# A fourth bank for the weight stream before the first attention, and modulation pieces moved between engines

## The reference, cut to what matters

```python
def first_block(...):                    # x: (1, 256, 1024) float32
    cond = jax.nn.silu(c)
    for l in range(DEPTH):               # DEPTH = 2
        mod = cond @ w_ada[l] + b_ada[l] # (1, 6 * 1024)
        sh1, sc1, g1, sh2, sc2, g2 = [m[:, None, :] for m in jnp.split(mod, 6, axis=-1)]
        h = _layer_norm(x) * (1.0 + sc1) + sh1
        mix = _mixer(h, w_in[l], ...)
        x = _layer_norm(DN_ALPHA * x + g1 * mix, ln1_g[l], ln1_b[l])
        h = _layer_norm(x) * (1.0 + sc2) + sh2
        ffn = _moe(h, w_router, router_bias, w_exp_gate[l], w_exp_up[l], w_exp_down[l])
        x = _layer_norm(DN_ALPHA * x + g2 * ffn, ln2_g[l], ln2_b[l])
    return x

def _mixer(h, w_in, qn_g, kn_g, w_pa, w_pb, w_o, cos, sin, slopes):
    proj = h @ w_in                      # 1024 -> 5120
    qa, ka, va, qd, kd, vd, gates = jnp.split(proj, IN_SPLITS, axis=-1)
    qa = _apply_rope(_rms_norm(qa, qn_g), cos, sin)
    ka = _apply_rope(_rms_norm(ka, kn_g), cos, sin)
    out_a = _global_gqa(qa, ka, va)
    ...                                  # out_b: three dilated groups, merged by their log-sums
    g_a, g_b = jnp.split(jax.nn.sigmoid(gates), 2, axis=-1)
    merged = g_a * (out_a @ w_pa) + g_b * (out_b @ w_pb)
    return merged @ w_o
```

## Time and profile before

| | us |
|---|---|
| median of 3 runs | 1646.46 |
| lowest, highest | 1646.29, 1647.08 |
| the profiled execution | 1647.17 |
| its span in the trace | 1645.4 |

### The profile page before, as it was taken

How to read it: one execution, slowest core, us unless ns; L and a number is a source line. 1 busy time by engine, 2 the same in 40 slices (tenths; PEclk the granted TensorE clock), 3 DMA queues, 4 the chain that set the end, 5 groups by cost and what they waited for, 6 DMA issues and landing times.

```text
span 1645.4 us, 16703 instructions
## 1 busy us (share of the span) xinstructions
PE 1516.3 (92%) x7088; PEld 856.8 (52%) x7088; DVE 532.2 (32%) x995; ACT 339.9 (21%) x735; POOL 178.4 (11%) x88
## 2 busy tenths in 40 slices
PE   5999889999789999989989998999988998999985
PEld 2777766444358777545436444434325764443322
DVE  2452235521366143551242034121104354221113
ACT  3113230312121223031123123111102243111101
POOL 0009970000000640000000000000002000000000
PEclk8999999799889999989989998999999999999998
DMA  9766453789646642379955524999998433899994
GB/s 387 291 268 243 158 220 139 295 349 418 288 155 262 236 190 103 135 299 375 416 232 204 180 103 160 424 425 427 428 427 352 154 112 149 338 427 428 427 428 197
DMA packets 34569, 462.71 MB, mean 281 GB/s; under 512 B 4432, under 2 KB 4560, under 8 KB 6160
## 3 DMA queue, kind: packets, MB, share of 16 engines
q1 hardware_dynamic: 31376, 447.34, 66.8%
q0 software_dynamic: 3104, 14.12, 2.7%
HBM read 458.29 MB, written 3.15 MB: 280 GB/s over the span
## 4 chain that ended last, share of the span: by engine, by line
PE 77%; DMA 15%; DVE 4%; ACT 1%; issue 1%; SPq 0%; DVEq 0%; ACTq 0%
PE work L739 15%; PE work L557 12%; DMA ring<-in_stream 9%; PE work L540 7%; PE work L792 7%; PE acc L557 7%; DMA area<-in_stream 6%; PE acc L540 5%; PE work L696 4%; PE acc L774 3%; PE work L549 3%; PE work L1218 2%; PE acc L1363 2%; PE work L1021 1%; PE work L757 1%
## 5 line engine op out<-in xcount | busy, mean ns | idle before, releaser
L739 PE MATMUL work<-ring,area 128*64 128x512 f32 x832 | 186.2, 594 | 10.7 <-DMA ring<-in_stream 10.6
L557 PE MATMUL work<-ht_sb,ring 128*128 128x256 f32 x640 | 145.0, 387 | 1.3 <-DMA ring<-in_stream 1.3
L557 PEld LDWEIGHTS work<-ht_sb,ring 128*128 128x128 f32 x640 | 122.9, 194 | 23.4 <-issue 4.4
L739 PEld LDWEIGHTS work<-ring,area 128*64 128x64 f32 x832 | 58.4, 137 | 129.7 <-issue 108.6
L557 PE MATMUL acc<-ht_sb,ring 128*128 128x256 f32 x512 | 115.7, 385 | 4.4 <-DMA ring<-in_stream 4.4
L2343 DVE SCALAR_TENSOR_TENSOR area<-area,comb_slot,work 128x256 f32<-128x256 f32 (+1 forms) x32 | 19.6, 614 | 299.1 <-ACT area L1586 299.1
L557 PEld LDWEIGHTS acc<-ht_sb,ring 128*128 128x128 f32 x512 | 97.3, 192 | 20.9 <-DMA ring<-in_stream 4.8
L739 PE MATMUL work<-area 128*64 128x512 f32 x448 | 100.9, 594 | 7.2 <-DMA area<-in_stream 7.1
L2355 DVE TENSOR_TENSOR area_r<-work,area_r 128x512 fp32r<-128x512 f32 x64 | 44.3, 692 | 173.2 <-ACT area_r L1594 140.7
L475 POOL TENSOR_TENSOR ring<-ring,silu_c 128x4096 f32<-128x4096 f32 x10 | 70.2, 7016 | 180.6 <-DMA ring<-in_stream 180.6
L792 PE MATMUL work<-area 128*64 128x512 f32 x384 | 89.2, 607 | 0.0
(11 more groups left out here) (318 smaller groups left out, 1930.3 us busy)
## 6 DMA issues: line engine op xcount, KB each, us to landing
ring<-in_stream SPq DMA_DIRECT2D x138, 2048.0 KB, 11.7
area<-in_stream SPq DMA_DIRECT2D x55, 2048.0 KB, 12.4
cst<-in_stream SPq DMA_DIRECT2D x19, 2048.0 KB, 16.8
ln_sb<-in_ln_vecs POOLq DMA_DIRECT2D x8, 1024.0 KB, 11.3
rel_rows<-mt_sb POOLq DMA_DIRECT2D x1, 2048.0 KB, 50.8
cst<-in_consts POOLq DMA_DIRECT2D x1, 1465.5 KB, 8.7
x_sb<-in_x SPq DMA_DIRECT2D x1, 1024.0 KB, 16.0
area<-rel_rows POOLq DMA_DIRECT2D x8, 128.0 KB, 2.9
```

What stands on the lines that cost most here:

```text
L557: ins = pe.matmul(dst, w[:, k, c0:c0 + n], src[:, k0 + k, :], start=k == 0, stop=k == ks - 1)
L739: ins = pe.matmul(banks[half][e * CAP:(e + 1) * CAP, :], tokens[:, k, at:at + CAP], w[:, kk, e, half * W:(half + 1) * W], start=k == 0, st ...
```

## The change

- A fourth bank exists from slot 0 until slot 16. It lies in the columns 1792 to 5888 of `area`, and ScalarE waits ahead of the copy of `gate(0)` until its last slot has been released.
- Seven pieces instead of five stand between the blocks of the input projection of layer 0, one behind block 0, two behind block 1, two behind block 2, one each behind blocks 3 and 4. VectorE sums them: pieces 1 and 2 ahead of the first rope, 3 and 4 between the ropes, 5 and 6 behind the second.
- VectorE also sums the first piece of the attention, piece 7, ahead of its first `max_a`. GpSimd sums four pieces, 8 to 11, instead of seven.
- TensorE finishes three pieces between the attention's steps instead of five; behind blocks 2 and 3 it finishes two pieces each. The last two still go behind the output projection.
- The first loads name their banks by table, since slot 0 is now in the fourth bank.

Layer 1 keeps its lists. From slot 26 on the banks follow each other as before, under other names.

The slots are now: 4 to 16 blocks and seven pieces (4 block 0, 5 piece 0, 6 block 1, 7 and 8 pieces 1 and 2, 9 block 2, 10 and 11 pieces 3 and 4, 12 block 3, 13 piece 5, 14 block 4, 15 piece 6, 16 block 5); 17 piece 7; 18 gate slot 0; 19 piece 8; 20 gate slot 1; 21 piece 9; 22 gate slot 2; 23 piece 10; 24 gate slot 3; 25 piece 11; 26 to 29 as before. The fourth bank holds slots 0, 4, 8, 12 and 16.

```diff
@@ -57,15 +57,16 @@
-ADA_BEHIND_IN = [[0, 1, 2, 3, 4], [0, 1, 2, 3, 4]]
-ADA_SUMMED_AFTER_IN = [[1, 2, 3, 4, 5], [1, 2, 3, 4, 5]]
+ADA_BEHIND_IN = [[0, 1, 1, 2, 2, 3, 4], [0, 1, 2, 3, 4]]
+ADA_SUMMED_AFTER_IN = [[1, 2, 2, 3, 3, 4, 5], [1, 2, 3, 4, 5]]
+ADA_AROUND_ROPE = [((1, 2), (3, 4), (5, 6)), ((1, 2), (3,), (4,))]
...
 ATTENTION_SLOTS = [
-    (("ada", 0), ("gate", 0), ("ada", 1), ("gate", 1), ("ada", 2), ("ada", 3), ("gate", 2), ("ada", 4), ("gate", 3),
-     ("ada", 5), ("ada", 6)),
+    (("ada", 0), ("gate", 0), ("ada", 1), ("gate", 1), ("ada", 2), ("gate", 2), ("ada", 3), ("gate", 3), ("ada", 4)),
     (("ada", 0), ("gate", 0), ("ada", 1), ("gate", 1), ("ada", 2), ("gate", 2), ("gate", 3))]
-ADA_AT_STEP = [5, 1]
+ADA_AT_STEP = [3, 1]
+ADA_BY_DVE = [1, 0]
 ADA_LATE = [10, 11]
@@ -123,7 +124,8 @@
-    return in_slot(l, ADA_BEHIND_IN[l][i]) + 1
+    b = ADA_BEHIND_IN[l][i]
+    return in_slot(l, b) + 1 + i - ADA_BEHIND_IN[l].index(b)
@@ -182,7 +184,8 @@
                    (SLOTS["moe2"] + 4, SLOTS["v"]), (SLOTS["moe3"] + 4, N_SLOTS)),
-        RING + 2: ((SLOTS["gla_in"] + 3, N_SLOTS),)}
+        RING + 2: ((SLOTS["gla_in"] + 3, N_SLOTS),),
+        RING + 3: ((0, SLOTS["ada0_0"]),)}
 BANKS = RING + len(OPEN)
@@ -261,6 +264,7 @@
         ring.append(cst[:, CONST["bucket"][0]:CONST["bucket"][0] + SLOT])
+        ring.append(area[:, 1792:1792 + SLOT])
@@ -424,10 +428,10 @@
             sp.dma_start(cst[:, 0:N_EARLY], consts[:, 0:N_EARLY]).then_inc(first_loaded, 16)
-            sp.dma_start(slot(0)[:, :], stream[0, :, :]).then_inc(slot_loaded[0], 16)
-            sp.dma_start(slot(1)[:, :], stream[1, :, :]).then_inc(slot_loaded[1], 16)
+            sp.dma_start(slot(0)[:, :], stream[0, :, :]).then_inc(slot_loaded[RING_BANK[0]], 16)
+            sp.dma_start(slot(1)[:, :], stream[1, :, :]).then_inc(slot_loaded[RING_BANK[1]], 16)
             sp.dma_start(X, x.rearrange("(t p) d -> p t d", p=P)).then_inc(inputs_loaded, 16)
-            sp.dma_start(slot(2)[:, :], stream[2, :, :]).then_inc(slot_loaded[2], 16)
+            sp.dma_start(slot(2)[:, :], stream[2, :, :]).then_inc(slot_loaded[RING_BANK[2]], 16)
             for s in range(RING, N_SLOTS):
@@ -455,9 +459,9 @@
-            pool.wait_ge(slot_loaded[0], 16 * 2)
+            pool.wait_ge(slot_loaded[RING_BANK[3]], 16 * nth_round(3))
             pool.dma_start(row[:, :], rows).then_inc(rows_loaded, 16)
-            pool.wait_ge(slot_loaded[2], 16 * 2)
+            pool.wait_ge(slot_loaded[RING_BANK[5]], 16 * nth_round(5))
             pool.dma_start(vec[:, :], bass.AP(vecs.tensor, 0, [[0, P], [1, N_VECS]])).then_inc(tables_loaded, 16)
@@ -492,7 +496,7 @@
             for l in range(DEPTH):
-                for i in range(len(ADA_IN_MIXER[l]) - len(ADA_BEHIND_IN[l])):
+                for i in range(ADA_BY_DVE[l], len(ADA_IN_MIXER[l]) - len(ADA_BEHIND_IN[l])):
                     ada(l, i)
@@ -926,8 +930,9 @@
             def ada_after_in(l, b):
-                if b in ADA_SUMMED_AFTER_IN[l]:
-                    layer, n = ADA_IN_MIXER[l][ADA_SUMMED_AFTER_IN[l].index(b)]
+                for (layer, n), at in zip(ADA_IN_MIXER[l], ADA_SUMMED_AFTER_IN[l]):
+                    if at != b:
+                        continue
                     pe.wait_ge(ada_ready, C.seen(ada_ready))
@@ -1007,7 +1012,8 @@
                     if step < ADA_AT_STEP[l]:
-                        pe.wait_ge(ada_by_pool, C.seen(ada_by_pool))
+                        done = ada_ready if step < ADA_BY_DVE[l] else ada_by_pool
+                        pe.wait_ge(done, C.seen(done))
                         i, bank, filled = fill()
@@ -1670,10 +1676,12 @@
             def ada_after_in(l, b):
-                if b in ADA_SUMMED_AFTER_IN[l]:
+                for (layer, n), at in zip(ADA_IN_MIXER[l], ADA_SUMMED_AFTER_IN[l]):
+                    if at != b:
+                        continue
                     j = J.take()
                     act.wait_ge(bank_filled[j % 4], nth(j))
-                    ada_out(*ADA_IN_MIXER[l][ADA_SUMMED_AFTER_IN[l].index(b)], work[j % 4], bank_drained[j % 4], nth(j))
+                    ada_out(layer, n, work[j % 4], bank_drained[j % 4], nth(j))
@@ -1740,6 +1748,8 @@
+                    if l == 0 and i == 0:
+                        act.wait_ge(slot_used[RING + 3], RING_BANK.count(RING + 3))
                     bank, drained, _ = fill()
@@ -2426,8 +2436,8 @@
                 dve.wait_ge(var_ready, C.made(var_ready))
-                ada_behind_in(l, 1)
-                ada_behind_in(l, 2)
+                for i in ADA_AROUND_ROPE[l][0]:
+                    ada_behind_in(l, i)
                 dve.wait_ge(tables_loaded, 16 * 2)
@@ -2461,7 +2471,8 @@
                             dve.wait_ge(done, C.made(done))
-                    ada_behind_in(l, 3 + t)
+                    for i in ADA_AROUND_ROPE[l][1 + t]:
+                        ada_behind_in(l, i)
                 skip(3 + len(ADA_BEHIND_IN[l]))
@@ -2504,6 +2515,8 @@
+                for i in range(ADA_BY_DVE[l]):
+                    ada(SLOTS[f"ada{i}_{l}"], ada_before(l) + ada_index(l, i))
                 max_a(0)
@@ -2862,8 +2875,7 @@
             put(blocked(a["w_in"][l][:, b * W:(b + 1) * W]))
-            if b in ADA_BEHIND_IN[l]:
-                put_ada([ADA_IN_MIXER[l][ADA_BEHIND_IN[l].index(b)]])
+            put_ada([piece for piece, at in zip(ADA_IN_MIXER[l], ADA_BEHIND_IN[l]) if at == b])
         for what, i in ATTENTION_SLOTS[l]:
...
                 put(blocked(a["w_in"][l][:, (IN_SLOTS + i) * W:(IN_SLOTS + i + 1) * W]))
```

## The result

| | before | after |
|---|---|---|
| median, lowest to highest (7 runs each) | 1646.29, 1640.41 to 1647.08 | 1628.60, 1627.20 to 1638.52 |
| ratio after / before | | 0.991, 95% interval 0.9894 to 0.9926 |
| profiled execution, its span | 1647.17, 1645.4 | 1629.47, 1627.7 |

The changed kernel is faster, by 14.8 us as the ratio has it (12 to 17 by its interval). Over all runs of this study the kernel before has 91, from 1637.2 to 1650.6 with a median of 1644.0, and the changed kernel 11, with a median of 1628.6: 15.4 us. A time of one trace and a median are not the same thing here: the profiled executions of the two kernels lie 17.7 us apart.

A forecast was written before the change was run, and what follows sets the result against it. TensorE, busy 92% of the span, was taken to lose time in two stream waits in layer 0's attention; -11.3 for the earlier branch start and -0.7 for clock gave -12.0, from 1646.46 to 1634.5 us, range 1631.5 to 1638.5.

The forecast's parts named there:

- The schedule: Layer 0's slot loads and pieces: gate(4)'s wait goes, 1.5 of 6.56 us stays; branch projections start 11.3 us earlier.
- the first maximum: VectorE in layer 0: piece 7 ends at 125.4, the maximum is due at 143.0, cover 17 us.
- Their clock: Branch projections: 1.47 us of lost clock regained if the clock holds; half taken, -0.7 us.
- all later stages should move as a block: Output projection, experts and everything later keep banks and releases, so they only shift along, adding no further gain.
- A: Later stages fall differently against clock changes: 1638 to 1640 with more drops, 1631 to 1633 with fewer; chance 0.16.
- B: Input projection: the wait moves to block 3, 2.2 us late plus 1.7 of clock, giving 1638.4; chance 0.07.
- C: gate(4): GpSimd's piece 8 starts so late that the first wait stays, 6.16 us not gained, 1640.7; chance 0.02.
- D: Projections: later landings of deciding loads cancel the gain from 6.3 us extra, slower beyond 8.0; chance 0.03.
- E: VectorE's piece 7 and GpSimd block each other over SBUF, first maximum 6 us late, 1640.5; chance 0.02.

The follow-up runs named there:

- e1: The changed kernel without the fourth bank, three banks throughout: 1642.7 us, ratio to before 1.000.
- e2: The kernel before with the fourth bank alone, its pieces and orders unchanged: 1644.2 us, ratio to before 1.0012.
- e9: The kernel before with unused matmuls filling TensorE's two waits, ahead of gate(4) and the branch projections: 1635.5 us, ratio 0.9954.
- e13: The kernel before with both TensorE waits filled by unused matmuls, run a second time: 1635.9 us, ratio 0.9947.
- e15: The changed kernel with 14 unused matmuls (12.4 us) ahead of layer 0's output projection: 1638.5 us, ratio to before 0.9968.

## Why the prediction was right or wrong

**The schedule was right, place by place.** `gate(4)` without a wait; 1.47 us instead of 6.56 ahead of the branch projections (forecast 1.5); start at 229.74 (229.4); VectorE's and GpSimd's pieces within 1.2 us of the forecast; no wait at blocks 3 and 4; the first maximum with 17.75 us of cover (17). e1 and e2 confirm it from the other side: each part alone gives what the same bookkeeping gives for it, a forecast of 13.7 us of new waits and lost clock for e1 (14.5 by its rows, 1642.7 - 1628.6 = 14.1 by the medians), none gained for e2. The places are those of one trace each: other executions of the same program came to `gate(4)` up to 2.6 us earlier.

**The step that failed is "Their clock", and with it "all later stages should move as a block".** I entered the clock as what two rows show behind two waits, 1.78 and 0 to 1.47 us, and took it for zero elsewhere. The waits themselves are worth 4.38 + 5.09 = 9.5 us of the 15.4, and about 6 remain, more than twice the 2.5 in my sum. Some 3 of them are the two local losses: the clock held at the branch projections too, so that the output projection starts 12.4 us earlier and not 12.0. The other 3 us of the medians (5.3 in the two traces) come behind it, in the stages that I moved as a block at a cost of nothing. In the traces they are 2.8 us at the start of layer 1, 1.5 in a row of the first experts (both clock) and 1.4 at the end of the kernel, about half of it a shorter idle time of TensorE (1.87 against 2.59 us) whose cause is not shown; other places give 0.4 back. That the start of layer 1 keeps the clock because it now lies earlier fits 17 of 18 traces and is not proven. e9 and e13 do show that something behind the stage changes when the stage does: their 9.2 and 9.1 us are far more than the 1.5 gained there. They do not show that it is all clock, as 2.7 us of it come at the end, where the idle time is gone. In e15, whose schedule gains nothing, what is left beyond that is not clear of nothing.

**The base was a second error.** The forecast started from the median of three runs, 1646.46, and I took three executions within 0.8 us for steadiness. 91 runs of the same kernel reach from 1637.2 to 1650.6 with a median of 1644.0. From that base my gain of 12 would have given 1632.0, 3.4 above what was measured.

**Rivals.** A, the clock in the later stages, named the right place with the wrong bounds: I gave it two or three drops more or one or two fewer, 1631 to 1640, and did not think of the idle time at the end. B, C and D did not happen: blocks 2 to 5 never waited, slot 22 landed in time, and a DMA share of 0.9 was not enough to make the deciding loads late. E did not either: piece 7 took 6.1 us as all others and ended at 125.4, six microseconds before GpSimd's first. But my sentence that no row of before shows such an overlap was wrong. In layer 0 behind the output projection both kernels have one. L2153 (L2143 in before) reads two SBUF tiles, once for each token tile: alone it takes 1.28 us, beside GpSimd's L495 2.29, and it ends 1.1 us after GpSimd's operation, which is what a lock held by GpSimd's operation would give. Both are the same in before (2.29 us at 296.67), so it is no part of the gain. The changed kernel:

```profile
268.94 1.28 DVE L2153 SCALAR_TENSOR_TENSOR xn_sb<-x_sb,mean_var,ln_sb 128x1024 f32<-128x1024 f32 x1
...
282.94 2.50 POOL L495 TENSOR_TENSOR xn_sb_r<-xn_sb,mt_sb_r 128x1024 fp32r<-128x1024 f32 x1 [60.07 <-ACT mt_sb_r L1539]
284.23 2.29 DVE L2153 SCALAR_TENSOR_TENSOR xn_sb<-x_sb,mean_var,ln_sb 128x1024 f32<-128x1024 f32 x1
```

The Trainium skill (TensorE: Matmul & The Clock Gate, Why this matters for your kernels) warns only of longer pauses than those at stake here. At the branch projections, behind 1.47 us, the clock held as that would have it; at layer 1's wait of 0.9 to 1.4 us it was down in eleven traces and up in seven, so the length of the pause does not decide by itself.

## What to carry to other kernels

When a ring of banks feeds several readers, follow each bank back to the engine that releases it: the slowest holder (here 15.5 us on GpSimd) sets the time of the next load, and an extra bank helps only together with an order that lets the late loads go early. The schedule of slots, worked out from the durations of one trace, was good to a microsecond. The gain in time was not: what lies behind the changed stage does not simply move along, and here it was worth another 3 us. Take the base from enough runs: three that agree said little here. And unused work is no clean control: it fills a wait, but it also moves every later instruction, and here that alone took away 2.7 us at the end of the kernel.

## What the runs showed of the hardware

- The same program on one core takes from 1637.2 to 1650.6 us in 91 executions, and the mean granted clock goes with it (0.955 to 0.964 in 23 of them). The changed kernel's 11 runs reach from 1627.2 to 1638.5, ten of them below 1630.
- Keeping TensorE at useless work in two waits (4.4 and 6.6 us) made the kernel 9 us faster, twice. In each trace the stage itself got 1.5 us of clock from it, because part of the loss came back elsewhere (15.75 us for 14.06 in e9, 22.64 for 20.96 in e13), and 2.7 us go with an idle time that is no longer there at the end.
- TensorE has idle times of up to 3.4 us in the experts for which the profile shows no cause. The last of them is there in all nine traces with at most one unused matmul and in none of the nine with two or more.
- The same matmuls at the start of layer 1 take 2.7 us more or less, and in 17 of 18 traces this goes with the time at which they start.
- Against 1628.6, useless work of 0.9 us cost 5.1 us, of 2.7 us 3.5 us; a wait of 1.5 us removed gave nothing that could be measured.
- A VectorE operation of 128x1024 with two SBUF inputs takes 1.28 us alone and 2.29 us when it starts while GpSimd runs one that reads SBUF too (L2153 and L495).
